# Two hybrid attention layers: attention of head pairs placed between the projection blocks

## The reference

```
h = rms_norm(x, pre_g) * (1 + scale) + shift
qa, ka, va, ga, qb, kb, vb, gb = split(h @ w_in)      # 8 parts of 512 columns
qa, ka, qb, kb = rope on 16 of the 64 features of each head
o_a = dilated_mixture_attention(qa, ka, va) * silu(ga)  # heads 0 to 7
o_b = moba_attention(qb, kb, vb) * silu(gb)             # heads 8 to 15
y = concat(o_a, o_b) @ w_out
x = x + gate * rms_norm(y, post_g)
```

## Time and profile before

| | us |
|---|---|
| three runs | 2271.99, 2274.67, 2266.93 |
| median | 2271.99 |
| profiled execution, its own time | 2276.18 |
| its span in the trace | 2274.3 |
| TensorE busy, whole span | 2016.8 (89%) |
| VectorE busy | 1289.0 (57%) |
| ScalarE busy | 976.8 (43%) |
| GpSimd busy | 241.6 (11%) |
| mean granted clock of TensorE | 0.914 of 2.4 GHz |

### The profile page before, as it was taken

The page is one execution under the profiler, slowest core; times in us unless marked ns, Lnnn a source line. Parts: engine busy times, 40 slices in busy tenths (PEclk is TensorE's granted clock), DMA queues, the critical chain, the costliest instruction groups (busy, mean ns, idle before and its releaser), DMA issues. The chain is left out here.

```text
span 2274.3 us, 47035 instructions
## 1 busy us (share of the span) xinstructions
PE 2016.8 (89%) x20403; PEld 1839.3 (81%) x20403; DVE 1289.0 (57%) x1847; ACT 976.8 (43%) x1420; POOL 241.6 (11%) x212
## 2 busy tenths in 40 slices
PE   2886989999989999898999968869999989997996
PEld 2775979999956999887799957759799989766966
DVE  3467436665553665476666554584366655655563
ACT  3442335444332544354654433523354434443453
POOL 1005300000020000013000010053000001101200
PEclk8898999999977999899999988889999989968967
DMA  3340015555653555355455523400145536413510
GB/s 93 109 142 2 5 57 167 186 189 184 200 176 112 170 187 186 113 167 179 131 183 188 181 75 109 146 2 4 58 150 188 189 123 193 148 34 103 168 56 19
DMA packets 286052, 288.39 MB, mean 127 GB/s; under 512 B 13128, under 2 KB 284088, under 8 KB 285720
## 3 DMA queue, kind: packets, MB, share of 16 engines
q1 hardware_dynamic: 285848, 285.39, 39.1%
HBM read 284.32 MB, written 1.05 MB: 125 GB/s over the span
## 5 line engine op out<-in xcount | busy, mean ns | idle before, releaser
L405 DVE TENSOR_TENSOR wl<-raw,wh 128x1024 fp32r<-128x1024 f32 x484 | 612.2, 1272 | 584.4 <-ACT wh L395 567.4
L360 PE MATMUL ps<-HH,wh 128*128 128x256 f32 x2336 | 672.7, 288 | 54.7 <-DVE HL L1601 43.0
L395 ACT ACTIVATE wh<-raw 128x1024 fp32r<-128x1024 f32 x484 | 501.7, 1043 | 502.9 <-PE ps L362 343.4
L361 PE MATMUL ps<-HL,wh 128*128 128x256 f32 x2336 | 660.8, 283 | 0.0
L362 PE MATMUL ps<-HH,wl 128*128 128x256 f32 x2336 | 657.8, 282 | 0.0
L360 PEld LDWEIGHTS ps<-HH,wh 128*128 128x128 f32 x2336 | 446.7, 191 | 67.9 <-DVE HL L1601 29.9
L361 PEld LDWEIGHTS ps<-HL,wh 128*128 128x128 f32 x2336 | 447.7, 192 | 3.3 <-issue 3.1
L362 PEld LDWEIGHTS ps<-HH,wl 128*128 128x128 f32 x2336 | 447.1, 191 | 0.0
L360 PE MATMUL ps<-XH,wh 128*128 128x256 f32 x768 | 222.7, 290 | 22.9 <-DVE XL L1601 22.9
L361 PE MATMUL ps<-XL,wh 128*128 128x256 f32 x768 | 221.1, 288 | 0.0
L362 PE MATMUL ps<-XH,wl 128*128 128x256 f32 x768 | 220.4, 287 | 0.0
(11 more groups left out here) (267 smaller groups left out, 2899.1 us busy)
## 6 DMA issues: line engine op xcount, KB each, us to landing
raw<-in_ffn_w_gu_dram SPq DMA_DIRECT2D x88, 1024.0 KB, 5.1
raw<-in_ffn_w_down_dram SPq DMA_DIRECT2D x32, 1024.0 KB, 5.1
raw<-in_w_in_dram SPq DMA_DIRECT2D x32, 1024.0 KB, 5.4
raw<-in_rw_w_rkv_dram SPq DMA_DIRECT2D x24, 1024.0 KB, 5.8
B<-in_w_ada_dram SPq DMA_DIRECT2D x24, 1024.0 KB, 7.3
raw<-in_ds_w_in_dram SPq DMA_DIRECT2D x14, 1024.0 KB, 5.2
raw<-in_ffn_w_down_dram SPq DMA_DIRECT2D x16, 768.0 KB, 4.7
raw<-in_sb_w_qkv_dram SPq DMA_DIRECT2D x12, 1024.0 KB, 5.2
```

Source lines behind the costliest of these rows:

```text
L360: e.matmul(om, h_[:, k, c], xh_, start=m == 0 and k0 + k == 0, stop=False, skip_group_check=True)
L361: e.matmul(om, h_[:, k, c], xl_, start=False, stop=False, skip_group_check=True)
L395: e.activation(wh[:, u % UNITS, 0:kn * 256], raw[:, j % RAW, k0 * 256:(k0 + kn) * 256], ACT.Copy).then_inc(*up("hi"))
L405: e.tensor_tensor(wl[:, u % UNITS, 0:kn * 256], raw[:, j % RAW, k0 * 256:(k0 + kn) * 256], wh[:, u % UNITS, 0:kn * 256].bitcast(F32), ALU. ...
```

## The change

It concerns the two hybrid layers alone.

- The blocks are ordered by heads: q, k, v of heads 0 to 3, then of heads 4 to 7, and so on, and the four G blocks last. plan_hybrid loads the weights in that order, in the same 20 pieces.
- The attention is done by *pairs* of heads (p = 0 to 7), and its pieces stand between the blocks: scores(p) for both heads, the matmuls of the one on partitions 0 to 63 next to those of the other on 64 to 127; turn(p), six transposes; values(p). VectorE's soft(p) and norm(p) and ScalarE's exps(p), turned(p) and out(p) stand in their own lists between the calls of lo and hi. Two buffers of pairs replace five of heads.
- The rotary turn: VectorE multiplies the block's result, straight from PSUM, by the sine (into a buffer that the rot2 matmul reads) and by the cosine (into q or k), and after the matmul adds its result. ScalarE no longer copies q and k, GpSimd does nothing of it.
- The maxima and the reciprocal of two heads are one instruction each.
- O is gated and split in four parts, two of them before the last G block ends.
- The barriers (L, 0), (L, 1) and (L, 2) are gone; single waits stand in their place.

The diff, cut to its core:

```diff
         def plan_hybrid(layer):
             first_piece["hy", layer] = len(plan)
-            for c in range(8):
-                plan_w(A["w_in_2"][layer], c * 512, 2)
+            places = [(c, g) for g in range(4) for c in range(3)] + [(3, g) for g in range(4)]
+            for c, g in places:
+                plan_w(A["w_in_2"][layer], (g // 2) * 2048 + c * 512 + (g % 2) * 256, 1)
             plan_w(A["w_out_2"][layer], 0, 4)
...
         def pe_hybrid(e, layer):
             L = ("hy", layer)
-            barrier(e, "mm", (L, 0))
             q_, k_, V = FM(1), FM(4), TM(5)
+            pr = [BUF[7][:, s_ * 768:s_ * 768 + 768].rearrange("p (u x) -> p u x", u=2) for s_ in range(2)]
+            pT = [BUF[8][:, s_ * 768:s_ * 768 + 768].rearrange("p (u x) -> p u x", u=2) for s_ in range(2)]
             pe_rms(e, (L, "rms"), None, ("f", 3) if layer == 0 else ("y", 0))
             mark("mm", ("tables", L))
             mark("unit", ("tables", L))
             h = parts_of(HH, HL)
-            pending = []
-            def run(i):
-                if pending:
-                    name, dst, g = pending.pop(0)
-                    pe_rope(e, (L, "rope " + name, g), dst[:, 2 * g:2 * g + 2, :], "rot2", 2, ("act", (L, name, g)))
-            for half in range(2):
-                for name, dst in (("q", q_), ("k", k_)):
-                    for g in (2 * half, 2 * half + 1):
-                        fm_block(e, (L, name, g), KD, h, [[("pool" if k % 2 else "dve", (L, "hl", k))] for k in range(KD)] if (half, name, g) == (0, "q", 0) else None,
-                                 ("act", (L, name, g)))
-                        run(0)
-                    pending += [(name, dst, 2 * half), (name, dst, 2 * half + 1)]
-                for g in (2 * half, 2 * half + 1):
-                    tm_block(e, (L, "v", g), h, None, ("act", (L, "v", g)))
-                    run(0)
-                for g in (2 * half, 2 * half + 1):
-                    fm_block(e, (L, "G", g), KD, h, None, ("act", (L, "G", g)))
-                    run(0)
-            assert not pending
-            barrier(e, "mm", (L, 1))
-            pe_softmax_attn(e, L, q_, k_, V)
-            barrier(e, "mm", (L, 2))
+            def block(name, g, engine="dve"):
+                first = (name, g) == ("q", 0)
+                (tm_block if name == "v" else fm_block_8)(e, (L, name, g), h, [[("pool" if k % 2 else "dve", (L, "hl", k))] for k in range(KD)] if first else None,
+                                                          (engine, (L, name, g)))
...
+            def rope(name, g, slot):
+                o = bank(e, (L, "rope " + name, g), ("dve", (L, "rope " + name, g)))
+                e.wait_ge(*at("dve", (L, "sin " + name, g)))
+                e.matmul(o[:, :], C("rot2"), FM(12)[:, 2 * slot:2 * slot + 2, :], start=True, stop=True,
+                         skip_group_check=True).then_inc(*up("mm", (L, "rope " + name, g)))
+            def scores(p):
+                os = [bank(e, (L, "qk", p, u), ("dve", (L, "lg", p, u))) for u in range(2)]
+                for name in ("q", "k"):
+                    e.wait_ge(*at("dve", (L, "rope " + name, p // 2)))
+                for u in range(2):
+                    e.matmul(os[u][:, 0:128], q_[half(u), p, 0:128], k_[half(u), p, 0:128], start=True, stop=True, skip_group_check=True)
+                for u in range(2):
+                    e.matmul(os[u][:, 128:384], q_[half(u), p, 128:256], k_[half(u), p, :], start=True, stop=True,
+                             skip_group_check=True).then_inc(*up("mm", (L, "qk", p, u)))
+            def turn(p):
+                e.wait_ge(*at("dve", (L, "pr", p)))
+                for u in range(2):
+                    o = bank(e, (L, "tr", p, u), ("act", (L, "pT", p, u)))
+                    for c in range(3):
+                        i = e.transpose(o[:, c * P:c * P + P], pr[p % 2][:, u, c * P:c * P + P], ident)
+                    i.then_inc(*up("mm", (L, "tr", p, u)))
+            def values(p):
+                o = bank(e, (L, "pv", p), ("act", (L, "pv", p)))
+                e.wait_ge(*at("act", (L, "v", p // 2)))
+                e.wait_ge(*at("act", (L, "pT", p, 1)))
+                for u in range(2):
+                    hd = (2 * p + u) * HD
+                    e.matmul(o[half(u), 0:256], V[:, 0, hd:hd + HD], pT[p % 2][:, u, 0:256], start=True, stop=False, skip_group_check=True)
+                for u in range(2):
+                    hd = (2 * p + u) * HD
+                    i = e.matmul(o[half(u), 128:256], V[:, 1, hd:hd + HD], pT[p % 2][:, u, 256:384], start=False, stop=True, skip_group_check=True)
+                i.then_inc(*up("mm", (L, "pv", p)))
+            block("q", 0)
+            block("k", 0)
+            rope("q", 0, 0)
+            block("v", 0, "act")
+            rope("k", 0, 1)
+            block("q", 1)
+            scores(0)
+            block("k", 1)
+            rope("q", 1, 2)
+            scores(1)
+            turn(0)
...
+            block("G", 2, "act")
+            turn(7)
+            values(6)
+            block("G", 3, "act")
+            values(7)
...
+            def value_block(g):
+                e.wait_ge(*at("unit", (L, "v", g)))
+                e.activation(V[:, :, g * 256:g * 256 + 256], PS(L, "v", g)[:, :].rearrange("p (j c) -> p j c", j=2), ACT.Copy).then_inc(*up("act", (L, "v", g)))
+            def block(name, g, dst, f=ACT.Copy):
+                e.wait_ge(*at("unit", (L, name, g)))
+                e.activation(dst[:, 2 * g:2 * g + 2, :], two(PS(L, name, g)[:, :]), f).then_inc(*up("act", (L, name, g)))
+            def exps(p):
+                s_ = p % 2
+                st = stats(s_)
+                e.wait_ge(*at("dve", (L, "nm", p)))
+                if p >= 2:
+                    e.wait_ge(*at("mm", (L, "tr", p - 2, 1)))
+                for u in range(2):
+                    for j, c in ((0, slice(0, 128)), (1, slice(128, 384))):
+                        n_ = 2 * j + u
+                        i = e.activation(pr[s_][:, u, c], lg[s_][:, u, c], ACT.Exp, scale=0.125, bias=st[:, 4 + n_:5 + n_], accum_out=st[:, 8 + n_:9 + n_])
+                i.then_inc(*up("act", (L, "exp", p)))
...
+            hi(e)
+            hi(e)
+            hi(e)
+            value_block(0)
...
+            hi(e)
+            block("G", 2, G, ACT.Silu)
+            turned(7)
+            out(6)
+            gated(0)
+            gated(1)
+            hi(e)
+            block("G", 3, G, ACT.Silu)
+            out(7)
+            gated(2)
+            gated(3)
+            log_and_exp(e)
...
+            def block(name, g, dst, slot):
+                o = two(PS(L, name, g)[:, :])
+                e.wait_ge(*at("unit", (L, name, g)))
+                e.tensor_tensor(FM(12)[:, 2 * slot:2 * slot + 2, :], o, angles(sin2), ALU.mult).then_inc(*up("dve", (L, "sin " + name, g)))
+                e.tensor_tensor(dst[:, 2 * g:2 * g + 2, :], o, angles(cos2), ALU.mult).then_inc(*up("dve", (L, name, g)))
+            def rope(name, g, dst):
+                x = dst[:, 2 * g:2 * g + 2, :]
                 key = (L, "rope " + name, g)
-                dve_rope(e, key, len(ropes) % 4, sin2, 2, *([("pool", ropes[-4])] if len(ropes) >= 4 else []))
-                ropes.append(key)
-            for half in range(2):
-                a, b = 2 * half, 2 * half + 1
-                lo(e, 6)
-                rope("q", a)
-                lo(e)
-                rope("q", b)
-                lo(e)
-                rope("k", a)
-                lo(e)
-                rope("k", b)
-                lo(e, 4)
+                e.wait_ge(*at("dve", (L, name, g)))
+                e.wait_ge(*at("mm", key))
+                e.tensor_tensor(x, x, two(PS(*key)[:, :]), ALU.add).then_inc(*up("dve", key))
+            def soft(p):
+                s_ = p % 2
+                st = stats(s_)
+                if p >= 2:
+                    e.wait_ge(*at("act", (L, "exp", p - 2)))
+                for u in range(2):
+                    e.wait_ge(*at("mm", (L, "qk", p, u)))
+                    e.tensor_tensor(lg[s_][:, u, :], PS(L, "qk", p, u)[:, 0:384], dil if p < 4 else cau, ALU.add).then_inc(*up("dve", (L, "lg", p, u)))
+                e.wait_ge(*at("dve", (L, "lg", p, 1)))
+                e.tensor_reduce(st[:, 0:2], lg[s_][:, :, 0:128], AX_X, ALU.max)
+                e.tensor_reduce(st[:, 2:4], lg[s_][:, :, 128:384], AX_X, ALU.max).then_inc(*up("dve"))
+                e.wait_ge(*now("dve"))
+                e.tensor_scalar(st[:, 4:8], st[:, 0:4], -0.125, None, ALU.mult).then_inc(*up("dve", (L, "nm", p)))
+            def norm(p):
+                s_ = p % 2
+                st = stats(s_)
+                e.wait_ge(*at("act", (L, "exp", p)))
+                e.reciprocal(st[:, 12:16], st[:, 8:12]).then_inc(*up("dve"))
+                e.wait_ge(*now("dve"))
+                for u in range(2):
+                    for j, c in ((0, slice(0, 128)), (1, slice(128, 384))):
```

(48 more changed lines are left out.)

158 lines of the change are left out of this document (130 added, 28 removed).

## The result

Each kernel ran on the same chip in turn. The median of four runs after the change is 2196.9 us (2195.3 to 2200.4), that of four before it 2269.5 us (2264.3 to 2274.7); the ratio is 0.968, with a 95% interval from 0.966 to 0.971. The change takes 72.5 us away. The forecast was 62 us less, to 2212, with a range from 2198 to 2236: the direction and the mechanism were right, and the time lies 1.1 us under the range's low end. The profiled execution took 2196.0 us (span 2194.1).

What follows compares the result with a forecast made beforehand. TensorE, by its low clock, bound the hybrid layers' attention. Per layer that became 19.3 + 2.6 + 2.0 + 1.4 = 25.3 us, with 2.3 us back in the output projection; together 62 us less, 2212, range 2198 to 2236.

Steps and rivals of the forecast that it cites:

- Pairs and breaks: Attention between blocks: 8 pairs at 2.41 us, 19.3 us, plus 2.6 us lost where small matmuls meet dense ones.
- Softmax in time: Before TensorE's turns: softmax fits with 0.2 to 1 us to spare, yet 2 us a layer added.
- Late wait: End of the attention: output projection waits for group 2 of the output, taken as 1.4 us.
- Clock of the output projection: Without the gap the output projection starts at 1.00; 2.3 us back in each layer.
- Barriers at the start: Removing the barrier at a layer's start gives nothing; it only repeats a chain of its own.
- rotary work without GpSimd: Rotary products moved from GpSimd to VectorE beside a busy TensorE: costed at nothing, covered by a block's 5.7 us.
- rival 3: Everything fits: no breaks, no waits but the last; 35 us gained in each layer, 2204; chance 0.08.
- no wait for weights between the blocks: In the interleaved stretch TensorE never waits for weights (lo); such a wait would make the prediction wrong.
- `lo` at 1.22 us without GpSimd: With GpSimd idle in the stretch, every lo on VectorE lasts 1.23 us.
- the clock at 1.00: Granted clock is 1.00 from a hybrid layer's second block to the end of its output projection.
- two heads side by side: Two scores matmuls of a pair start within 0.65 us, on the two halves of the rows.
- Rivals 1, 2 and 4: Softmax round trip sets pace, 2232, 0.15; clock falls between blocks, 2310, 0.05; two heads' scores do not overlap, 2229, 0.05.

Runs made afterwards that it cites:

- two forms with filling: Kernel before plus constant 128x512 matmuls that nothing uses: ten per hybrid layer, 2243.9 us; or five at the eighth head of the attention, 2261.7 us.

## Why the prediction missed, step by step

It named the right stage, mechanism and bound, and forecast 61.9 us between the rstds; 71.5 came. The median fell under the range. What was off were sizes, nearly all on one side, and a base that was too high:

- **Pairs and breaks** (19.3 + 2.6 = 21.9 us a layer): the visits sum to 20.9. The 0.4 us of the earlier trace rows holds for a lone visit of scores (1.06 = 0.65 + 0.4) and where scores meet values (1.86 against 1.45), but turns next to either cost what their parts say (1.66 against 1.61 and 1.76). 1.0 us a layer too much.
- **Softmax in time** (2.0 us a layer): 0. The step that failed is the rounding up of a positive margin into a wait. TensorE reached the first turn 7.5 us after the end of the scores, as worked out (7.2 to 7.5), and VectorE was done after 6.1, where the working had 6.3 to 7.0. The eight pairs had 0.45 to 2.16 us to spare; the prediction had 0.2 to 1 (its own numbers reach 7.5 - 6.3 = 1.2, and the two products of 0.68 us that it lets VectorE finish first would give 7.7, not 7.0). Its own working said that the softmax fits, and I charged it anyway. This is the largest single term, 4.0 us.
- **Late wait** (1.4): 0.82. The form was right, group 2's low part behind the last `lo`, but it is 0.6 us shorter; moving it away gave 0.8 and 0.5.
- **Clock of the output projection** (2.3 a layer): without its wait the projection now takes 22.6 us in both layers, against 25.4 and 25.2: 2.7 and 2.5.
- **Barriers at the start** (0): 0.8 + 1.2 = 2.0. "The barrier only repeats the chain" was wrong: the sums of squares that could have begun stood behind it.
- **Not in the sum:** the first 20.7 us of the blocks ran at a clock of 0.81 and 0.79 instead of 0.79 and 0.75. With it the two stretches of blocks took 0.6 and 1.3 us less than before the change. Most of it is likely the spread of single executions: from the rstd to the end of the last block the kernel before took 106.3 and 106.9 us, its two forms with filling 106.1 to 106.5, and the six forms with the new blocks and the pairs behind them 105.9 to 106.8. That also bears out the nothing at which the rotary work without GpSimd was costed.

Windows of the blocks' first 20.7 us, of both layers, before and then after:

```profile
1869.30:1890.00 20.70, 18.59 (x127) 17.83 (x128) 10.56 (x21) 7.91 (x13) 3.03 (x4) 0.79 0.50 161
2072.30:2093.00 20.70, 18.42 (x122) 17.85 (x123) 11.32 (x21) 8.01 (x13) 3.03 (x4) 0.75 0.52 163
```
```profile
1861.90:1882.60 20.70, 18.11 (x121) 16.87 (x122) 13.31 (x26) 6.94 (x11) 3.05 (x4) 0.81 0.51 161
2028.30:2049.00 20.70, 18.48 (x121) 17.25 (x122) 13.30 (x26) 7.05 (x11) 3.06 (x4) 0.79 0.52 163
```

Together 2.0 + 4.0 + 1.2 + 0.6 + 2.0 + 1.9 = 11.7 us more than forecast, 73.5 in all. The base was high as well: 2274 against a median of 2269.5 in the comparison, 4.5 us. The two add up to 16 us, of which a lower gain of the medians (72.5) gives one back: 2212 - 15 = 2197. The range reached 14 us below the forecast: to rival 3, "everything fits", and a little over its 4 us for the spread of the runs. Rival 3's own gain, 35 us a layer, is almost what came between the rstds (35.4 and 36.1), though partly by luck: its visits are 1.6 us a layer too cheap, and the clock and the blocks gave that back. What put the result under the range is outside its sum, the start (2.0 us) and the base (4.5 us).

The steps that held: no wait for weights between the blocks, `lo` at 1.22 us without GpSimd, the clock at 1.00 from 10.7 and 11.6 us after the layer's rstd on (within its first block), two heads side by side, and the cover of the rotary work. Rivals 1, 2 and 4 did not come; rival 3, everything fits, at 2204, was nearest, and had a chance of 0.08.

Where do the 35 to 36 us a layer come from? The pair code with its order, standing apart and with a clock that recovers, gave 18.7 and 20.5 (170.4 and 168.5). What only the blocks give is the other 16.7 and 15.6: VectorE's 3.3 us a pair, the first wait of 5.8 us and the 1.9 and 1.0 us at the end, with the slow start of the output projection behind them. The clock by itself, in the kernel before, was worth 15.1 where it held. These shares overlap, since an order without waits is also what holds the clock, so I don't add them.

## What to carry to other kernels

A stage that stands alone costs its latency, its clock and the slow start of the next stage; pieces between dense work cost little more than their own length. When it must stand alone, first look for a loop between two engines in the chain of waits and issue the producer ahead of the consumer: here that was worth more than keeping the clock by force. And where a worked margin is positive, forecast no wait, and put the doubt into the range.
